# A two-layer decoder trunk on one core: three weight units instead of two in the opening, k tile by k tile, and the first mean squares from the x columns

## The reference

```python
for l in range(DEPTH):                      # 2 layers
    h = h + 0.5 * rmsnorm(swiglu(rmsnorm(h, g[FFN1_PRE]), ffn_w_in[l, 0], ffn_w_out[l, 0]), g[FFN1_POST])
    hn = rmsnorm(h, g[MIX_PRE])             # then one wide product, a pooling mixer and a windowed attention
    ...
    h = h + rmsnorm(merged @ w_o[l], g[MIX_POST])
    h = h + 0.5 * rmsnorm(swiglu(rmsnorm(h, g[FFN2_PRE]), ffn_w_in[l, 1], ffn_w_out[l, 1]), g[FFN2_POST])

def swiglu(x, w_in, w_out):                 # w_in: 1024 x 2*2816, w_out: 2816 x 1024
    gate, up = jnp.split(x @ w_in, 2, axis=-1)
    return (jax.nn.silu(gate) * up) @ w_out
```

## Time and profile before

| | us |
|---|---|
| runs | 1190.59, 1191.3, 1193.52 |
| median | 1191.3 |
| the profiled execution's own time | 1191.37 |
| its span (first to last record) | 1189.3 |
| PE busy / DVE busy / ACT busy / POOL busy | 1179.4 / 712.3 / 541.1 / 457.9 |

### The profile page before, as it was taken

The page is one execution under the profiler, slowest core; times in us unless marked ns, Lnnn a source line. Parts: engine busy times, 40 slices in busy tenths (PEclk is TensorE's granted clock), DMA queues, the critical chain, the costliest instruction groups (busy, mean ns, idle before and its releaser), DMA issues.

```text
span 1189.3 us, 23831 instructions
## 1 busy us (share of the span) xinstructions
PE 1179.4 (99%) x9310; PEld 1149.5 (97%) x9310; DVE 712.3 (60%) x1050; ACT 541.1 (45%) x761; POOL 457.9 (39%) x521
## 2 busy tenths in 40 slices
PE   8999999999999999999999999999999999999997
PEld 7999999999999999999999999999999999999986
DVE  5755444868665865544477554447676658755542
ACT  6433334536553553333355333345466545544441
POOL 1855500207212476542128545112063124865600
PEclk9999999999999999999999999999999999999999
DMA  9754457373355355545636553573734653754540
GB/s 323 253 180 158 127 186 224 97 231 107 90 151 188 123 181 176 175 128 179 217 112 213 177 168 119 195 209 111 240 108 101 175 181 107 229 195 160 188 165 35
DMA packets 197997, 198.69 MB, mean 167 GB/s; under 512 B 4368, under 2 KB 190864, under 8 KB 197920
## 3 DMA queue, kind: packets, MB, share of 16 engines
q1 hardware_dynamic: 197600, 197.27, 52.4%
q10 hardware_dynamic: 320, 0.34, 0.1%
HBM read 196.54 MB, written 1.05 MB: 166 GB/s over the span
## 4 chain that ended last, share of the span: by engine, by line
PE 97%; DVE 2%; DMA 1%; SPq 0%; ACT 0%; issue 0%; DVEq 0%
PE bank L505 28%; PE bank L506 28%; PE bank L504 28%; PE bank L736 2%; PE bank L738 2%; PE bank L737 2%; PE bank L640 1%; PE bank L825 1%; PE bank L820 1%; PE bank L631 1%; PE bank L779 1%; PE bank L538 1%; DMA raw<-in_ffn_w_in 1%; PE bank L539 1%; PE bank L564 1%; PE bank L790 0%
## 5 line engine op out<-in xcount | busy, mean ns | idle before, releaser
L504 PE MATMUL bank<-x_hi,w_hi 128*128 128x272 f32 (+1 forms) x1988 | 572.1, 288 | 2.0 <-DVE w_lo L1607 1.4
L505 PE MATMUL bank<-x_lo,w_hi 128*128 128x272 f32 (+1 forms) x1988 | 570.5, 287 | 0.0
L506 PE MATMUL bank<-x_hi,w_lo 128*128 128x272 f32 (+1 forms) x1988 | 568.6, 286 | 0.0
L939 ACT ACTIVATE w_hi<-raw 128x2048 fp32r<-128x2048 f32 (+2 forms) x208 | 348.8, 1684 | 412.5 <-PE bank L506 398.3
L1240 DVE TENSOR_TENSOR w_lo<-raw,w_hi 128x2048 fp32r<-128x2048 f32 (+3 forms) x203 | 419.7, 2073 | 158.8 <-ACT w_hi L939 153.8
L504 PEld LDWEIGHTS bank<-x_hi,w_hi 128*128 128x128 f32 x1988 | 375.8, 189 | 4.0 <-DVE w_lo L1607 1.7
L505 PEld LDWEIGHTS bank<-x_lo,w_hi 128*128 128x128 f32 x1988 | 375.3, 189 | 0.3
L506 PEld LDWEIGHTS bank<-x_hi,w_lo 128*128 128x128 f32 x1988 | 373.7, 188 | 0.0
L1807 POOL TENSOR_TENSOR hid_hi<-silu,up_r 128x272 f32 x88 | 136.5, 1552 | 163.4 <-DVE up_r L1385 145.4
L505 PE MATMUL bank<-hid_lo,w_hi 128*128 128x272 f32 x528 | 152.3, 289 | 0.0
L506 PE MATMUL bank<-hid_hi,w_lo 128*128 128x272 f32 x528 | 151.9, 288 | 0.0
(11 more groups left out here) (205 smaller groups left out, 1276.4 us busy)
## 6 DMA issues: line engine op xcount, KB each, us to landing
raw<-in_ffn_w_in SPq DMA_DIRECT2D x86, 1024.0 KB, 5.1
raw<-in_w_in SPq DMA_DIRECT2D x24, 1024.0 KB, 5.7
raw<-in_ffn_w_out SPq DMA_DIRECT2D x24, 768.0 KB, 4.4
raw<-in_ffn_w_out SPq DMA_DIRECT2D x24, 640.0 KB, 4.0
raw<-in_ffn_w_out SPq DMA_DIRECT2D x10, 1024.0 KB, 5.0
raw<-in_w_in SPq DMA_DIRECT2D x16, 512.0 KB, 5.2
raw<-in_w_attn_proj SPq DMA_DIRECT2D x32, 256.0 KB, 4.6
raw<-in_w_o SPq DMA_DIRECT2D x8, 1024.0 KB, 5.7
```

The costliest lines, as they stand in the source:

```text
L504: pe.matmul(ps[:, t0:T], w[0], a_hi[:, t0:T], start=start, stop=False)
L505: pe.matmul(ps[:, t0:T], w[0], a_lo[:, t0:T], start=False, stop=False)
L506: return pe.matmul(ps[:, t0:T], w[1], a_hi[:, t0:T], start=False, stop=stop)
L939: last = act.activation(hi, w, ACT.Copy)
```

## The change

What it does:

- The opening takes three units (0, 1 and 2) at once, k tile by k tile, into six banks (`first_three`, `OPEN_BANKS`). The weights and columns come in five pieces (`OPEN_K`): one k tile, one, two, two, two. Unit 3 follows in two halves (`fourth_unit`).
- Norm gains and the weights of the first k tile are issued from ACT's queue, ahead of its table load; SP's queue begins with two columns pieces.
- The x rows and the meta rows are no longer loaded. POOL squares the x columns and adds them (`first_squares`: 8 products, 7 sums), and PE sums them with three matmuls (`sum_part`) ahead of k tile 6 of unit 0; the result is spread ahead of k tile 7 of unit 1.
- The warm-ups are 8 fp32 matmuls of 256 columns on a zeroed `r`, which DVE sets, in place of 2 of 512 and 3 of 256 on the identity, which POOL makes.
- Sinks and geometry are loaded from SP after unit 5; `layer_columns(0)` on DVE comes after the loop over the units.

The core of the diff:

```diff
-PIECES, PK = KD // 2, 2
+OPEN_K = (slice(0, 1), slice(1, 2), slice(2, 4), slice(4, 6), slice(6, 8))
+OPEN_UNITS = 3
+OPEN_BANKS = (3, 1, 6, 0, 4, 5)
+LAST_PIECE = len(OPEN_K) - 1
+FOURTH = (slice(0, KD // 2), slice(KD // 2, KD))
...
+def open_order(piece):
+    return (0, 2, 1) if OPEN_K[piece].stop == OPEN_K[piece].start + 1 else (0, 1, 2)
...
-            sp.dma_start(g_all[:, :], norm_columns).then_inc(norms_in, 16)
             first_w = ffn_w_in[0:1, 0].rearrange("o (k p) n -> p (o k) n", p=P)
-            first_to, second_to = (raw[:, u, :].rearrange("p (k c) -> p k c", c=UW) for u in range(2))
-            for piece in range(PIECES):
-                k = slice(PK * piece, PK * (piece + 1))
+            def columns(piece):
+                k = OPEN_K[piece]
                 sp.dma_start(h[:, k, :], x_columns[:, k, :]).then_inc(columns_in[piece], 16)
-                sp.dma_start(first_to[:, k, :], first_w[:, k, 0:UW]
-                             ).then_inc(raw_landed[0] if piece == PIECES - 1 else first_raw[piece], 16)
-                if piece % 2 == 1:
-                    k = slice(KD // 2 * (piece // 2), KD // 2 * (piece // 2 + 1))
-                    sp.dma_start(second_to[:, k, :], first_w[:, k, FF:FF + UW]
-                                 ).then_inc(second_raw if piece == 1 else raw_landed[1], 16)
+            def open_weights(piece):
+                k = OPEN_K[piece]
+                if k.stop == k.start + 1:
+                    kk = slice(k.start * UW, k.stop * UW)
+                    sp.dma_start(raw[:, 0:3:2, kk], first_w[:, k.start, 0:2 * UW].rearrange("p (u c) -> p u c", u=2)
+                                 ).then_inc(first_raw[piece][0], 16)
+                    sp.dma_start(raw[:, 1, kk], first_w[:, k.start, FF:FF + UW]).then_inc(first_raw[piece][1], 16)
+                    return
+                for u in range(OPEN_UNITS):
+                    c = u % 2 * FF + u // 2 * UW
+                    sp.dma_start(raw[:, u, :].rearrange("p (k c) -> p k c", c=UW)[:, k, :], first_w[:, k, c:c + UW]
+                                 ).then_inc(raw_landed[u] if piece == LAST_PIECE else first_raw[piece][u], 16)
+            for piece in range(len(OPEN_K)):
+                columns(piece)
+                if piece > 0:
+                    open_weights(piece)
+            for half, k in enumerate(FOURTH):
+                sp.dma_start(raw[:, 3, :].rearrange("p (k c) -> p k c", c=UW)[:, k, :], first_w[:, k, FF + UW:FF + 2 * UW]
+                             ).then_inc((fourth_raw, raw_landed[3])[half], 16)
...
-                    load(2, w1[:, :, UW:2 * UW])
-                    for b in range(2):
-                        sp.dma_start(first_x[:, b, :], x[0, b * P:(b + 1) * P, :]).then_inc(tokens_in[b], 16)
-                    load(3, w1[:, :, FF + UW:FF + 2 * UW])
                     for j in range(2):
                         slot_free(4 + j, 0)
                         load(4 + j, w1[:, :, j * FF + 2 * UW:j * FF + 3 * UW])
+                    sp.dma_start(sink_all[:, :], sinks.rearrange("(o l) h -> o (l h)", o=1).to_broadcast([P, DEPTH * HEADS])
+                                 ).then_inc(geo_in, 16)
+                    sp.dma_start(geo[:, :], geometry).then_inc(geo_in, 16)
...
+            def first_three():
+                def product(c, k, low_weights, operand, start=False, stop=False):
+                    return pe.matmul(bank[OPEN_BANKS[c]][:, 0:T], weights(c // 2, k, c % 2)[low_weights], operand[:, k, :],
+                                     start=start, stop=stop)
+                pe.wait_ge(xhi_ready, 1)
+                pe.wait_ge(first_hi, 1)
+                for c in range(2):
+                    product(c, 0, 0, x_hi, start=True)
+                x_tile(0, 0)
+                for c in range(2):
+                    product(c, 0, 0, x_lo)
+                pe.wait_ge(first_lo, 1)
+                for c in range(2):
+                    product(c, 0, 1, x_hi)
...
+                for k in range(KD):
+                    piece = [k in range(s.start, s.stop) for s in OPEN_K].index(True)
+                    if k > 0:
+                        x_tile(k, 0)
+                    for at, u in enumerate(open_order(piece)):
+                        if k + at == 0:
+                            continue
+                        if k == OPEN_K[piece].start:
+                            if piece == LAST_PIECE:
                                 unit_split(u, 0)
+                            else:
+                                pe.wait_ge(first_lo, OPEN_UNITS * piece + at + 1)
+                        if (k, u) == OPEN_SUM_AT:
+                            sum_part(0, 0, 0)
+                        if (k, u) == OPEN_SPREAD_AT:
+                            spread_rms(0, 0)
+                        for c in (2 * u, 2 * u + 1):
+                            last = products(bank[OPEN_BANKS[c]], weights(u, k, c % 2), x_hi[:, k, :], x_lo[:, k, :],
+                                            k == 0, k == KD - 1, 0)
+                            if k == KD - 1:
+                                last.then_inc(first_done if c % 2 == 0 else unit_done, 1)
...
-            pe.wait_ge(consts, 1)
+            pe.wait_ge(warm_ready, 1)
             for _ in range(WARM_FIRST):
-                pe.matmul(warm[:, :], ident[:, :], ident[:, :].unsqueeze(1).to_broadcast([P, 4, P]), start=True, stop=True)
-            for _ in range(WARM_SHORT):
-                pe.matmul(warm[:, 0:2 * P], ident[:, :], ident[:, :].unsqueeze(1).to_broadcast([P, 2, P]), start=True, stop=True)
+                pe.matmul(first_warm[:, 0:SEQ], r[:, 0:P], r[:, 0:SEQ], start=True, stop=True)
...
-            act.dma_start(first_meta, meta_tokens).then_inc(tokens_in[2], 16)
+            w_k0 = ffn_w_in[0, 0, 0:P, :]
+            act.dma_start(g_all[:, :], norm_columns).then_inc(norms_in, 16)
+            act.dma_start(raw[:, 0:3:2, 0:UW], w_k0[:, 0:2 * UW].rearrange("p (u c) -> p u c", u=2)).then_inc(first_raw[0][0], 16)
+            act.dma_start(raw[:, 1, 0:UW], w_k0[:, FF:FF + UW]).then_inc(first_raw[0][1], 16)
             act.preload_act_table(ACT.Silu)
...
+            for piece, ks in enumerate(OPEN_K):
                 act.wait_ge(columns_in[piece], 16)
-                first_operand(PK * piece)
-                first_operand(PK * piece + 1)
-                first_split(piece)
-                if piece % 2 == 1:
-                    second_split(piece // 2)
-            def first_halves(u):
-                act.wait_ge(raw_landed[u], landed_at(u, 0))
-                for piece in range(2):
-                    w, hi, _ = split_parts(u, 2)[piece]
-                    act.activation(hi, w, ACT.Copy).then_inc((first_hi, hi_done)[piece], 1)
-            first_halves(2)
-            for b in range(2):
-                token_sum(b, first_x[:, b, :])
-            act.dma_start(sink_all[:, :], sinks.rearrange("(o l) h -> o (l h)", o=1).to_broadcast([P, DEPTH * HEADS])
-                          ).then_inc(geo_in, 16)
-            act.dma_start(geo[:, :], geometry).then_inc(geo_in, 16)
-            first_halves(3)
+                for k in range(ks.start, ks.stop):
+                    first_operand(k)
+                for u in open_order(piece):
+                    open_split(u, piece)
+            fourth_split(0)
+            fourth_split(1)
...
+            dve.wait_ge(norms_in, 16)
+            for piece, ks in enumerate(OPEN_K):
+                dve.wait_ge(columns_in[piece], 16)
+                for k in range(ks.start, ks.stop):
+                    x_low(0, g_all, k)
+                for at, u in enumerate(open_order(piece)):
+                    open_split(u, piece, at)
+            fourth_split(0)
+            mean_square(0, 0)
+            fourth_split(1)
             dve.wait_ge(consts, 1)
...
+            def first_squares():
+                for piece, ks in enumerate(OPEN_K):
+                    pool.wait_ge(columns_in[piece], 16)
+                    for k in range(ks.start, ks.stop):
+                        if k >= 3:
+                            pool.wait_ge(acc_done, k - 2)
+                        to = acc[:, :] if k == 0 else sq[:, k % 2, :]
+                        pool.tensor_tensor(to, h[:, k, :], h[:, k, :], ALU.mult).then_inc(open_square, 1)
+                        if k >= 1:
+                            pool.wait_ge(open_square, k + 1)
+                            if k >= 2:
+                                pool.wait_ge(acc_done, k - 1)
+                            pool.tensor_tensor(acc[:, :], acc[:, :], sq[:, k % 2, :], ALU.add).then_inc(acc_done, 1)
...
-WARM_FIRST, WARM_SHORT = 2, 3
+WARM_FIRST = 8
+OPEN_SUM_AT, OPEN_SPREAD_AT = (6, 0), (7, 1)
```

More of the change, by code:

```diff
@@ L375, in split_parts, with open_parts @@
                     for t in range(2) for a in range(0, KD, k)]
+        def open_parts(u, k):
+            c = slice(k.start * UW, k.stop * UW)
+            return raw[:, u, c], w_hi[:, u, c], w_lo[:, u, c]
```

(7 more changed lines are left out.)

160 lines of the change are left out of this document (51 added, 109 removed).

## The result

The changed kernel takes 1192.21 us (median of 22 runs, 1191.32 to 1193.71), the kernel before 1190.57 (22 runs, 1189.76 to 1193.52). The ratio is 1.0016, 95% interval 1.0010 to 1.0022: the kernel is 1.2 to 2.6 us slower, less than the 0.3% that I had taken as the bound of what can be told, yet clearly on the other side of the 1.0 us that I had forecast it to win. Timed again later, the ratio was 1.0014 (1.0004 to 1.0023).

What follows compares the result with a forecast made beforehand. PE's opening was taken to bound the kernel, with 2.8 us of waits and restarts before unit 4. Unit 4 moving from 33.97 to 33.0 took 1.0 off 1191.37, giving 1190.4 us; range for 8 in 10: 1187.9 to 1193.0.

Steps and rivals of the forecast that it cites:

- The baseline: Whole kernel before the change: own time of the profiled execution 1191.37 us, taken as the median 1191.3.
- The start: PE's first product in the opening: set by the warm-ups, moving from 6.58 to 6.5 us, bounds 4.7 and 8.4.
- rival 3: Opening: warm-ups at the high clock and early first weights, start 5.1, 3.9 us won, 1187.4 us; chance 0.10.
- Three units a k tile: Opening on PE: 18 matmuls per k tile remove the old gaps; without waits unit 4 starts at 31.5, 2.5 us earlier.
- What POOL does to DVE: the price: Opening: POOL and DVE take turns on SBUF, one instruction each; a DVE instruction meeting POOL costs 0.51 us more.
- What POOL does to DVE: where it was put: Turns counted from 8.2 us; low weights of k tiles 2 and 3 each 0.3 to 0.5 late, PE at sum by 21.
- POOL's last sum decides: Ahead of k tile 6: POOL's last sum at 21.4 us barely holds PE, so unit 4 starts at 33.0, 1.0 earlier.
- an `acc` done by 19: Sign named beforehand: POOL's sums finished by 19 us instead of about 21.4 would point to turns costing little.
- rival 2: Opening: POOL's turns with DVE cost little, unit 4 at 31.5, 2.5 us won, 1188.8 us; chance 0.24.
- Rival 4: POOL's sum comes later than counted and PE waits: 1193.0 us at chance 0.12, 1196 at the upper bound, 0.06.
- Later steps: From unit 4 on: its low weights ready at 31.8 against 33.0 wanted, margin 1.2 us, no new wait.
- The sum: Whole kernel: the profiled 1191.37 us minus 1.0 won in the opening gives 1190.4.

Runs made afterwards that it cites:

- e7: Changed kernel with the eight squares moved from POOL to ACT and five warm-ups instead of eight; median 1188.92 us, 0.9983 of the kernel before.
- e1: Changed kernel without POOL's eight squares and seven sums (tile set to a constant, output not the reference's); median 1189.47 us, 0.9988 of the kernel before.
- e9: Changed kernel with sums of squares made by ACT from token rows and the spread moved into unit 3's first tile; 1188.50 us, 0.9981 of before.
- e12: Changed kernel with POOL's sums replaced by four independent squares that nobody reads (output not the reference's); median 1189.83 us, 0.9994 of the kernel before.
- e4: Changed kernel with POOL's squares of k tiles 2 to 7 held back and PE's sum two places later; 1192.95 us, 1.0016 of before.

## Why the prediction was right or wrong

**The baseline.** Right in form, 0.7 us off: I took 1191.3, the median of three runs and the time of the profiled execution. The median of 22 is 1190.57, and the second profile shows where most of the difference is: one stand in the opening, 1.6 or 0.8 us. The opening of one kernel varies between two executions by 0.7 us at unit 4 (33.97 and 33.26), half of what this change moves.

**The start (6.5).** Right: 6.60 in the first profile, and e7 shows that the warm-ups set it. But that it came within 0.1 is partly luck: 6.5 is near the middle of a spread, 6.07 to 7.25 over the ten profiles with eight warm-ups; rival 3 (a start at 5.1) has no execution.

**Three units a k tile (31.5 without hindrance).** Right: e1, with the sum on PE, reached 31.49, e9 without it 30.99, with no waits. With PE never kept waiting the new opening is worth about 2 us.

**What POOL does to DVE: the price.** Right. +0.51 for an instruction that meets POOL was read from one row; by the rows of the changed kernel and of e1 it is 0.45 for an `x_lo` (1.81 against 0.91 for two), 0.49 for a `w_lo` of 256 columns (2.56 against 1.09 for three) and 0.52 for one of 512 (3.46 against 1.90 for three), and in e12 0.43 for each operation of POOL. The turns hold too: from 7.8 to 17.2 us DVE makes ten instructions, and POOL begins ten. The section of the Trainium skill that I weighed, "Who interferes with whom" of "SBUF — State Buffer", is right that the two contend; that DVE is blocked for the whole of a POOL instruction is again not what the rows show: a POOL square, 0.64 alone, costs DVE 0.43 and takes 0.82 itself.

**What POOL does to DVE: where it was put.** This step failed: "So from 8.2 us on I count turns", and with it PE's arrival at the sum, "at 20.1 if nothing holds it, and up to 21 with `w_lo` of k tiles 2 and 3 each late by 0.3 to 0.5". It came there at 23.34. I charged one contested instruction to the piece that PE waits for. But DVE is one queue, and everything it makes from POOL's start on is late by the sum. POOL's squares of k tile 2 start at 7.5 (the columns landed 0.7 earlier than my interpolation), when DVE has yet to make all of k tile 1's low weights. Between there and PE's piece stand, against e1: three `w_lo` of k tile 1, +1.5; two `x_lo`, +0.9; and the piece itself, +0.5. That is 2.9 us, not 0.3 to 0.5. DVE began this stretch 0.2 earlier than in e1, so the piece is 2.7 later, 13.2 instead of 10.5. PE comes to it at 11.3, so 0.8 of that was free, and 1.9 had to show as a wait; with the restart of PE that is the stand of 2.1. I had left k tile 1's splits out of the count altogether. The pieces of k tiles 2 to 5, late in the same way, held PE up at three more places.

**POOL's last sum decides (21.4).** Wrong, and its cause is the same count from the other side: 12 operations from 7.54 to 18.9 are 0.95 each, I had 1.1. The sum is 2.5 us earlier than forecast and 4.5 before PE takes it. So "an `acc` done by 19", which I had named as the sign of rival 2 and a faster kernel, was seen, in a kernel that is slower: the sign looked at POOL's end and not at DVE's. Rival 4, the one that gave a slower kernel, priced exactly this chain; the kernel is slower, by another way. e4 shows that the rival's mechanism exists once POOL starts its last twelve operations 3.7 us later.

**Later steps.** Right: no wait from unit 4 on, the span behind it unchanged. The stand of 0.2 at unit 4 is gone, but the second profile of the kernel before doesn't have it either, so that isn't shown to be the change's doing.

**The sum.** Forecast for unit 4 33.0, measured 34.84 and 34.40. From the first product, 26.5 forecast, 28.2 and 27.2 measured. The range held 1192.2 only because it reached to rival 4's cases, which is luck: the kernel got there by another way, and the forecast itself had the wrong sign. Rival 2's 31.5 was reached only where POOL was emptied (e1), and there for another reason than that turns cost little.
